# The router's products inside a recurrence's loop: weights stationary, tokens moving, four chunks on four column tiles

## The chip, the cores and the metric

One core of a Trainium2 chip runs the whole program. The time is device microseconds from start to end of an execution; the median of three is compared. All data is fp32 in HBM.

## The reference

One step of a one-layer streaming encoder for 512 new frames and 64 frames of a running stream (576 tokens, 5 tiles of at most 128). Cut to its course:

```python
h = rmsnorm(x, norm1_g)
proj = h @ w_in
att, k_new, v_new = swa_sink_attention(qa, ka, va, k_hist, v_hist, pos0, attn_sink)
rec, s_new = hgrn2(qb, fb, ib, gb, lb, hgrn_norm_g, s0)   # chunkwise recurrence, 4 heads of 128
x = x + jnp.concatenate([att, rec], axis=-1) @ w_o
h2 = rmsnorm(x, norm2_g)
g_logits = h2 @ w_rg + b_rg            # 4 groups
e_all    = h2 @ w_re + b_re            # 4 experts in each group: 20 columns in all
# top-1 group, top-2 experts in it, softmax weights
x = x + hier_moe(h2)                   # 16 experts, each 1024 -> 256 -> 1024
y = rmsnorm(x, final_norm_g)
```

What matters here is `h2 @ [w_rg | w_re]`: for each tile of 128 tokens a product over 1024 features, in 8 chunks of 128, with 20 result columns.

## The kernel before

The program is written by hand, engine by engine: every engine has its own list of instructions, in the order in which the code issues them, and semaphores join the lists. Each engine works its list strictly from front to back.

First come the input projections, then attention by chunks of 64 frames. Then a loop over token tiles, `t = 1` to `4`, joins three things: the recurrence of tile `t`, the product with `w_o` of tile `t - 1` (`out_part`, 16 units of three matmuls each, split in pieces to fill PE's time), and the second norm and the router of tile `t - 2`. Behind the loop the last two tiles are routed, tokens are gathered by expert, and the experts run.

On PE, a pass of the loop is: `turn_rec(t - 1)` (transposes the recurrence's result, L1898), `decays(t)`, `out_part` units 0 to 6, `inner(t)` (L1861, L1866), `turn_h2(t - 2)` (L1957), units 6 to 10, `sums(t)` (L1880, L1889), `route(t - 2)` (L1971), units 10 to 16. `out_part(t - 1)` begins only when DVE's `mix_low(t - 1)` is done (`rec_taken`).

On ACT, behind `sums(t)`: `rec_squares(t)` (L956), then in the next pass `mix_high` (L1000, L1002), `second_norm` (L988), `cum_exps` (L944 to L947), and `h2T_half` (L993), which copies half of the transposed h2 out of PSUM.

On POOL: the reciprocal roots (`rstd`, L663, L664), of the recurrence's rows (`ro`) and of the second norm.

On DVE, a pass ends and the next begins so:

```python
inner_and_states(t)      # L1283, L1302
h2T_half(t - 2)          # L1348, the other half of h2T
add_out(t - 1, 0)        # L1272
logf_low(t + 1)
take_logits(t - 2)       # L1359, waits for the router's products
normed(t)                # L1315, waits for POOL's ro
gain(t + 1)              # L1244, not in the last pass
pick(t - 2)              # L1378 to L1395: ranks the 20 logits
# next pass
add_out(t - 1, 1)        # L1272; t here is the new one less one
mix_low(t)               # L1453, L1456, waits for ACT's mix_high
```

Behind the loop PE issues five small products that rank the picked tokens (L1992, L1996), and then `out_part` of the last tile (its first matmul is L1942).

PSUM bank 7 holds both the router's logits (20 columns) and, in `inner`, the state update of a tile's first chunk, which DVE reads in `inner_and_states`; `route` therefore waits for `state_ready`. fp32 products are two records each on PE in the trace.

Of the kernel before, what the change touches and what calls it, by code (L numbers as in the profile page):

```python
# [24 lines left out]
ALU = mybir.AluOpType  # L25
ACT = mybir.ActivationFunctionType
# [5 lines left out]
P = 128  # L32
D = 1024
KC = D // P
SEQ, DEC = 512, 64
TOK = SEQ + DEC
NT = (TOK + P - 1) // P
PROMPT_TILES = SEQ // P
CHUNK = 64
NCHUNK = TOK // CHUNK  # L40
# [5 lines left out]
BW = BH * BK  # L46
EPS = 1e-6
NG, EPG = 4, 4
NE = NG * EPG
# [25 lines left out]
def rows_of(t):  # L75
    return min(P, TOK - t * P)
# [44 lines left out]
def program(nc, io):  # L121
    ctx = ExitStack()
    with ctx:
        def sem(name):
            return ctx.enter_context(nc.semaphore(name))
# [7 lines left out]
        def place(name, shape, dt=F32):  # L133
            n = int(np.prod(shape[1:])) * 4
            t = nc.alloc_sbuf_tensor_at(name, shape, dt, offset=cursor[0])
            cursor[0] += (n + 31) // 32 * 32
            return t
# [3 lines left out]
        ident = place("ident", [P, P])  # L141
# [13 lines left out]
        g2_bc = place("g2_bc", [P, D])  # L155
        ng_at = cursor[0]
        ng_bc = place("ng_bc", [P, BW])
        w_route = place("w_route", [P, KC, NG + NE])
        b_route = place("b_route", [P, NG + NE])
        sink_bc = place("sink_bc", [P, GROUP])  # L160
        stats = place("stats", [P, 6, 8])
# [105 lines left out]
        def hgrn_buffers(t):  # L267
# [8 lines left out]

        St = [hT_flat[:, 6 * BW:7 * BW], kT[:, 0:BW], V[:, 0:BW // KVW, :].rearrange("p t k -> p (t k)")]
        logf_parts = at("logf_parts", [P, 2, BW], F32R, hT_at + 7 * BW * 4)
        s_sample = bias[:, :, :].rearrange("p m k -> p (m k)")[:, 0:BW]

# [83 lines left out]
        h2_stored = sems("h2_stored", NT)  # L366
        h2_turned, h2T_act, h2T_dve, logits_ready, logits_taken = (
            sem(n) for n in ("h2_turned", "h2T_act", "h2T_dve", "logits_ready", "logits_taken"))
        route_diff, route_exp, picks_ready, rank_ready, hot_ready, slots_ready = (
            sem(n) for n in ("route_diff", "route_exp", "picks_ready", "rank_ready", "hot_ready", "slots_ready"))  # L370
        over_hot_ready, over_slots_ready, over_ready = (
# [268 lines left out]
        def _(pool):  # L640
# [86 lines left out]
            for c in range(NCHUNK):  # L727
                if c >= 2:
                    pool.wait_ge(scores_ready, c - 1)
                for b in range(KV):  # L730
# [3 lines left out]

                    pool.wait_ge(qbd_ready, KV * c + b + 1)

            for t in range(NT):
                rstd(0, t, BH, 1.0 / BK, osq_ready, ro_ready, osq[:, :], ro[:, :], rows_of(t))
                if t:
                    rstd(1, t - 1, 1, 1.0 / D, ssq2_ready, rstd2_ready)  # L740
# [83 lines left out]
        def _(act):  # L824
# [125 lines left out]
            def rec_squares(t):  # L950
                r = rows_of(t)
                act.wait_ge(rec_sum, t + 1)
                for h in range(BH):
                    cols = slice(h * BK, (h + 1) * BK)

                    last = act.activation(logf[0:r, t, cols], ps[0:r, 5, cols], ACT.Square,  # L956
                                          accum_out=osq[0:r, h:h + 1])
                last.then_inc(osq_ready, 1)
# [32 lines left out]
            def h2T_half(t):  # L991
                act.wait_ge(h2_turned, t + 1)
                act.activation(h2T[:, 0:512], bank(turned_bank(t)), ACT.Copy).then_inc(h2T_act, 1)  # L993
                if t >= NT - 2:
                    act.activation(h2T[:, 512:1024], bank(turned_bank(t) + 1), ACT.Copy).then_inc(h2T_act, 1)

            def mix_high(t):
                r = rows_of(t)
                act.wait_ge(rec_turned, t + 1)
                act.activation(mix_hi[:, BH:KC, 0:r], bank(6).rearrange("p (h t) -> p h t", h=BH)[:, :, 0:r],  # L1000
                               ACT.Copy).then_inc(mix_hi_done, 1)
                act.activation(mix_hi[:, 0:BH, 0:r], mixT[:, 0:BH, tok(t)], ACT.Copy).then_inc(mix_hi_done, 1)  # L1002
# [7 lines left out]
            for t in range(1, NT):  # L1010
                mix_high(t - 1)
                if t == 1:
                    high(len(W_GROUPS), 6, KC)
                else:
                    second_norm(t - 2)
                cum_exps(t)
                if t < NT - 1:
                    logf_high(t + 1)
                if t == 1:
                    high(len(W_GROUPS) + 1, 0, KC)  # L1020
                else:
                    h2T_half(t - 2)
                rec_squares(t)
            mix_high(NT - 1)
            second_norm(NT - 2)
# [42 lines left out]
            for t in range(NT):  # L1068
                r = rows_of(t)
# [615 lines left out]
        def _(pe):  # L1685
# [184 lines left out]
            def sums(t):  # L1870
                r = rows_of(t)
                _, _, qex, aT, _, _ = hgrn_buffers(t)
                pe.wait_ge(at_ready, t + 1)
                if t == NT - 1:
                    pe.wait_ge(s_in, 16)
                elif r > CHUNK:
                    pe.wait_ge(state_ready, 2 * t + 1)
                for h in range(BH):
                    cols = slice(h * BK, (h + 1) * BK)
                    pe.matmul(ps[0:r, 5, cols], aT[0:r, h, 0:r], vf[0:r, t, cols], start=h == 0, stop=True,  # L1880
                              skip_group_check=h > 0)

                for h in range(BH):
                    cols = slice(h * BK, (h + 1) * BK)
                    for c in range(r // CHUNK):
                        before = s_sample if t == NT - 1 else St[(2 * t + c) % 3]
                        rows = slice(c * CHUNK, (c + 1) * CHUNK)
                        if 2 * t + c:
                            last = pe.matmul(ps[rows, 5, cols], qex[:, h, rows], before[:, cols], start=False,  # L1889
                                             stop=True, skip_group_check=True)  # L1890
                last.then_inc(rec_sum, 1)
# [31 lines left out]
            def out_part(t, first, last_n):  # L1923

                r = rows_of(t)
                for n in range(first, last_n):
                    half, c = n // KC, n % KC
                    k = len(W_GROUPS) + half
                    if t == 0:
                        pe.wait_ge(w_lo_done, KC * k + c + 1)  # L1930
                    if c == 0:
                        if t == 0:
                            wait_emptied(pe, "g")
                            wait_emptied(pe, "b")
                        else:
                            pe.wait_ge(x2_ready, 2 * (t - 1) + half + 1)
                        pe.wait_ge(rec_taken, t + 1)
                    out, w_h, w_l = ps[0:r, half, :], w_high(k, c), w_lo[k % RING][:, c, :]
                    if t == NT - 1:
                        if c:  # L1940
                            pe.matmul(out, mix_hi[:, c, 0:r], w_l, start=False, stop=False)
                        last = pe.matmul(ps[:, half, :], mix_hi[:, c, :], w_h, start=c == 0, stop=c == KC - 1)  # L1942
                        if c == 0:
                            pe.matmul(out, mix_hi[:, c, 0:r], w_l, start=False, stop=False)
                    else:
                        pe.matmul(out, mix_hi[:, c, 0:r], w_h, start=c == 0, stop=False)  # L1946
                        pe.matmul(out, mix_hi[:, c, 0:r], w_l, start=False, stop=False)  # L1947
                        last = pe.matmul(out, mix_lo[:, c, 0:r], w_h, start=False, stop=c == KC - 1)  # L1948
                    if c == KC - 1:
                        last.then_inc(out_ready, 1)  # L1950
# [9 lines left out]

            def route(t):
                r = rows_of(t)
                pe.wait_ge(h2T_act, t + 1 + max(t - NT + 3, 0))
                if t < NT - 2:
                    pe.wait_ge(h2T_dve, t + 1)
                if t:
                    pe.wait_ge(logits_taken, t)

                pe.wait_ge(state_ready, min(2 * t + 5, 2 * PROMPT_TILES + 1))
                for c in range(KC):  # L1970
                    last = pe.matmul(ps[0:r, 7, 0:NG + NE], h2T[:, c * P:c * P + r], w_route[:, c, :],  # L1971
                                     start=c == 0, stop=c == KC - 1)
                last.then_inc(logits_ready, 1)

            for t in range(1, NT):
                early, late = (6, 12) if t == 1 else (6, 10)
                turn_rec(t - 1)
                decays(t)  # L1980
                out_part(t - 1, 0, early)
                inner(t)
                if t >= 2:
                    turn_h2(t - 2)
                out_part(t - 1, early, late)
                sums(t)
                if t >= 2:
                    route(t - 2)
                out_part(t - 1, late, 2 * KC)

            def rank_before(t):
# [22 lines left out]
                rank_own(t)  # L2014
            out_part(NT - 1, 0, 2 * KC)
            turn_h2(NT - 2)
            route(NT - 2)
            turn_h2(NT - 1)
            route(NT - 1)
            for t in range(NT - 3):  # L2020
                slots_of(t)
            pe.wait_ge(picks_ready, NT - 1)
# [122 lines left out]
```

## Time and profile before

| | |
|---|---|
| median of 3 runs | 491.68 us (491.62 to 493.36) |
| the profiled execution's own time | 491.68 us |
| its span, first to last instruction | 489.9 us |
| PE busy | 440.4 us, 90% |
| DVE busy | 250.1 us, 51% |
| ACT busy | 156.5 us, 32% |
| POOL busy | 91.9 us, 19% |
| PE, 40 products L1971 (five routings) | 9.3 us |
| granted clock of PE, 218 to 281 us | 1.00 |

Times are microseconds from the span's start. PE is matmul, PEld its weight loads, which run beside it. A matmul's end is modelled, and neighbouring matmuls overlap in the records; in the chain each is given the time until the next. "[idle before <-releaser]" is how long the engine stood idle ahead of the instruction, and who ended it. The passes of the loop that route a tile (t = 2, 3, 4) lie between 218 and 281 us.

### The profile page before, as it was taken

What the parts mean: (1) busy time and instruction counts of PE and PEld (TensorE: products, weight loads), DVE (VectorE), ACT (ScalarE), POOL (GpSimd) and SP (SyncE); (2) the same over time, 40 slices, a digit from 0 to 9 for tenths busy, and PEclk for the clock granted to TensorE, in tenths of its full rate; (3) what the DMA queues carried; (4) which work ended last, traced back from release to release, by engine and by line L of the source; (5) the groups of instructions that cost most, each with busy time, mean ns of one, the idle gap of its engine ahead of it and who ended that gap; (6) DMA issues with size and microseconds to landing.
All of it is one profiled execution on the core that took longest, in us unless ns stands there. A gap on an engine that the chain in (4) does not pass through costs nothing.

```text
span 489.9 us, 7956 instructions
## 1 busy us (share of the span) xinstructions
PE 440.4 (90%) x3093; PEld 304.1 (62%) x3093; DVE 250.1 (51%) x597; ACT 156.5 (32%) x355; POOL 91.9 (19%) x156
## 2 busy tenths in 40 slices
PE   6999899999999999999999989799999999998200
PEld 5879799887999678778888868333333433433000
DVE  4877715378568436776756468333312112111086
ACT  6664540375244653832413230111011111111021
POOL 4239100201000001010100023201211122122044
PEclk9999999999999999999999995999999999999755
DMA  8905401303000940051011099999999999950394
GB/s 299 224 16 174 172 9 26 146 1 137 36 2 9 255 153 1 22 173 44 0 44 66 1 349 418 343 415 343 397 372 399 424 413 417 416 212 34 122 343 180
DMA packets 31823, 93.18 MB, mean 190 GB/s; under 512 B 8969, under 2 KB 12177, under 8 KB 25649
## 3 DMA queue, kind: packets, MB, share of 16 engines
q1 hardware_dynamic: 27728, 82.81, 46.4%
q0 software_dynamic: 4064, 9.97, 5.3%
q8 instruction: 19, 0.31, 0.3%
q14 instruction: 12, 0.09, 0.1%
HBM read 85.75 MB, written 11.80 MB: 199 GB/s over the span
## 4 chain that ended last, share of the span: by engine, by line
PE 78%; DVE 10%; DMA 6%; ACT 3%; issue 1%; POOL 1%; SPq 0%; POOLq 0%; DVEq 0%; ACTq 0%
PE ps L2085 17%; PE ps L2064 8%; PE ps L1733 8%; PE ps L1735 7%; PE ps L1734 7%; PE ps L1946 3%; PE ps L2039 3%; PE ps L1948 3%; PE ps L1947 3%; DMA pair<-y_pairs 2%; DVE x L1664 2%; PE ps L1971 2%; DMA h_rows<-s_buf 1%; PE ps L1779 1%; ACT s_buf L927 1%
## 5 line engine op out<-in xcount | busy, mean ns | idle before, releaser
L2085 PE MATMUL ps<-we_gu,xT 128*32 128x512 f32 x768 | 84.9, 594 | 0.7 <-ACT xT L1038 0.6
L2085 PEld LDWEIGHTS ps<-we_gu,xT 128*32 128x32 f32 x768 | 24.5, 110 | 52.3 <-issue 50.2
L1733 PE MATMUL ps<-hT_hi,w_hi 128*128 128x288 f32 x160 | 48.5, 303 | 1.6 <-DVE w_lo_q L1108 0.8
L2064 PE MATMUL ps<-we_d,hhT 128*32 128x512 f32 x384 | 43.5, 592 | 1.3 <-DVE hhT L1649 1.3
L1640 DVE TENSOR_TENSOR hh<-sg,ps 128x256 f32<-128x256 f32 x12 | 5.1, 421 | 70.3 <-ACT sg L1054 70.3
L1733 PE MATMUL ps<-w_hi,hT_hi 128*128 128x512 f32 x96 | 38.8, 405 | 0.1
L1734 PE MATMUL ps<-w_lo,hT_hi 128*128 128x512 f32 x96 | 37.5, 390 | 0.0
L1733 PEld LDWEIGHTS ps<-hT_hi,w_hi 128*128 128x128 f32 x160 | 30.1, 188 | 5.0 <-issue 2.5
L1054 ACT ACTIVATE sg<-ps 128x256 f32<-128x256 f32 x12 | 4.6, 384 | 86.6 <-PE ps L2085 86.6
L2064 PEld LDWEIGHTS ps<-we_d,hhT 128*32 128x32 f32 x384 | 13.0, 110 | 29.0 <-issue 29.0
L854 ACT ACTIVATE w_hi<-ring,g_col 128x512 fp32r<-128x512 f32 (+1 forms) x48 | 28.7, 678 | 0.1
L1735 PE MATMUL ps<-hT_hi,w_lo 128*128 128x288 f32 x96 | 28.3, 295 | 0.0
L1111 DVE SCALAR_TENSOR_TENSOR w_lo<-ring,g_col,w_hi 128x512 fp32r<-128x512 f32 (+1 forms) x40 | 25.4, 701 | 0.0
L1625 DVE COPY y<-ps 128x512 f32<-128x512 f32 x12 | 8.3, 692 | 33.4 <-PE ps L2064 33.4
L1947 PE MATMUL ps<-w_lo,mix_hi 128*128 128x512 f32 x64 | 25.0, 390 | 0.0
L1734 PE MATMUL ps<-hT_lo_a,w_hi 128*128 128x288 f32 x80 | 23.6, 295 | 0.0
L1734 PE MATMUL ps<-hT_lo_b,w_hi 128*128 128x288 f32 x80 | 23.6, 295 | 0.0
L732 POOL COPY qbd<-qa 64x256 f32<-64x256 f32 x18 | 8.0, 444 | 80.6 <-PE ps L1779 44.7
L663 POOL TENSOR_SCALAR ms<-osq 128x4 f32<-128x4 f32 (+1 forms) x5 | 1.0, 193 | 110.6 <-ACT logf L956 110.6
L1733 PEld LDWEIGHTS ps<-w_hi,hT_hi 128*128 128x128 f32 x96 | 18.0, 188 | 5.7 <-issue 1.2
L2039 PEld LDWEIGHTS ps<-ident,xg 128*128 128x128 f32 x104 | 12.6, 194 | 13.1 <-issue 10.1
L1734 PEld LDWEIGHTS ps<-w_lo,hT_hi 128*128 128x128 f32 x96 | 18.1, 188 | 3.2
(389 smaller groups left out, 957.7 us busy)
## 6 DMA issues: line engine op xcount, KB each, us to landing
we_gu<-in_w_gate SPq DMA_DIRECT2D x16, 1024.0 KB, 9.2
we_gu<-in_w_up SPq DMA_DIRECT2D x16, 1024.0 KB, 11.0
we_d<-in_w_down SPq DMA_DIRECT2D x16, 1024.0 KB, 10.5
ring<-in_w_in SPq DMA_DIRECT2D x4, 2048.0 KB, 7.9
pair<-y_pairs SPq DMA_DIRECT2D x8, 512.0 KB, 7.6
ring<-in_w_in SPq DMA_DIRECT2D x3, 1024.0 KB, 8.2
x_first<-in_x_p SPq DMA_DIRECT2D x4, 512.0 KB, 9.8
x<-in_x_p SPq DMA_DIRECT2D x4, 512.0 KB, 3.7
```

Source lines behind the costliest of these rows:

```text
L854: act.activation(w_split(k, w_high(k, c)), w_raw(k, c), ACT.Copy, scale=gain).then_inc(w_hi_done, 1)
L1111: ins = dve.scalar_tensor_tensor(out, w_raw(k, c), g1_col[:, c:c + 1], hi, ALU.mult, ALU.subtract)
L1664: dve.scalar_tensor_tensor(x[0:r, t, :], pair[0:r, t, i * D:(i + 1) * D], gates[0:r, i, t:t + 1], x[0:r, t, :], ALU.mult, ALU.add).then_in ...
L1733: pe.matmul(out, stationary[0], moving[0], start=c == 0, stop=False)
L1734: pe.matmul(out, stationary[0], moving[1], start=False, stop=False)
L1735: last = pe.matmul(out, stationary[1], moving[0], start=False, stop=c == KC - 1)
L1946: pe.matmul(out, mix_hi[:, c, 0:r], w_h, start=c == 0, stop=False)
L1947: pe.matmul(out, mix_hi[:, c, 0:r], w_l, start=False, stop=False)
L1948: last = pe.matmul(out, mix_lo[:, c, 0:r], w_h, start=False, stop=c == KC - 1)
L2039: last = pe.transpose(ps[:, 1 + half, (c % 4) * P:(c % 4 + 1) * P], xg[:, b, c:D:KC], ident[:, :])
L2064: last = pe.matmul(ps[cols, 4 + 2 * (b % 2) + half, :], hhT[:, f, cols], we_d[u][:, f, 512 * half:512 * half + 512], start=f == 0, stop=f ...
L2085: last = pe.matmul(ps[cols, 0, :], xT[:, c, cols], we_gu[u][:, :, c, :], start=c == 0, stop=c == KC - 1)
```

## The change

In the three passes of the loop with a router, `route` no longer holds h2T (128 features x 128 tokens) as the stationary operand with the 20 weight columns moving. A chunk's weights are stationary, 32 columns read from a flat buffer (20 of the chunk, 12 of what follows), and the 128 tokens move. Chunks 0 to 3, then 4 to 7, go to four column tiles, so that four partial sums stand on partitions 0 to 31, 32 to 63 and so on of bank 7. ACT copies these out of PSUM (`take_parts`), and one more product (`route_sum`) with `pick_row`, a 128x20 matrix of ones and zeros, adds the four and gives the logits with tokens on partitions, as before. `route` moves ahead of `sums(t)`; `route_sum` stands behind it. The two routings behind the loop (`route_last`) stay as they were. POOL builds `pick_row` and clears the 12 added columns.

```diff
-        w_route = place("w_route", [P, KC, NG + NE])
+        w_route_flat = place("w_route_flat", [P, KC * (NG + NE) + 12])
...
+        bias_flat = bias[:, :, :].rearrange("p m k -> p (m k)")
+        s_sample = bias_flat[:, 0:BW]
+        parts, pick_row = bias_flat[:, BW:BW + P], bias_flat[:, BW + P:BW + P + NG + NE]
+        w_route = w_route_flat[:, 0:KC * (NG + NE)].rearrange("p (c n) -> p c n", c=KC)
...
+            pool.memset(w_route_flat[:, KC * (NG + NE):], 0.0)
+            pool.wait_ge(scores_taken, NCHUNK)
+            chain(pool.tensor_tensor(pick_row, ident[:, 0:20], ident[:, 32:52], ALU.add))
+            chain(pool.tensor_tensor(pick_row, pick_row, ident[:, 64:84], ALU.add))
+            chain(pool.tensor_tensor(pick_row, pick_row, ident[:, 96:116], ALU.add))
+            pool.sem_inc(consts, 1)
...
+            def take_parts(t):
+
+                r = rows_of(t)
+                act.wait_ge(parts_ready, t + 1)
+                if t:
+                    act.wait_ge(logits_ready, t)
+                act.activation(parts[:, 0:r], ps[:, 7, P:P + r], ACT.Copy).then_inc(parts_taken, 1)
...
                     h2T_half(t - 2)
+                    take_parts(t - 2)
                 rec_squares(t)
...
             def route(t):
                 r = rows_of(t)
-                pe.wait_ge(h2T_act, t + 1 + max(t - NT + 3, 0))
-                if t < NT - 2:
-                    pe.wait_ge(h2T_dve, t + 1)
+                pe.wait_ge(h2T_act, t + 1)
+                pe.wait_ge(h2T_dve, t + 1)
                 if t:
                     pe.wait_ge(logits_taken, t)
 
-                pe.wait_ge(state_ready, min(2 * t + 5, 2 * PROMPT_TILES + 1))
+                pe.wait_ge(state_ready, 2 * t + 5)
+                if t == 0:
+                    pe.wait_ge(consts, 3)
+                for k in range(2):
+                    for j in range(4):
+                        c = 4 * k + j
+                        last = pe.matmul(ps[32 * j:32 * j + 32, 7, P:P + r], w_route_flat[:, 20 * c:20 * c + 32], h2T[:, c * P:c * P + r],
+                                         start=k == 0, stop=k == 1)
+                last.then_inc(parts_ready, 1)
...
+            def route_sum(t):
+
+                r = rows_of(t)
+                pe.wait_ge(parts_taken, t + 1)
+                pe.matmul(ps[0:r, 7, 0:NG + NE], parts[:, 0:r], pick_row,
+                          start=True, stop=True).then_inc(logits_ready, 1)
...
                 out_part(t - 1, early, late)
+                if t >= 2:
+                    route(t - 2)
                 sums(t)
                 if t >= 2:
-                    route(t - 2)
+                    route_sum(t - 2)
                 out_part(t - 1, late, 2 * KC)
```

On PE, in the pass t = 3 of the loop, this is the end of `out_part`'s units 6 to 10, `sums(3)` and `route(1)` before.

```order
L1946 MATMUL ps<-wo_hi_h,mix_hi 128x512
L1947 MATMUL ps<-w_lo_106,mix_hi 128x512
L1948 MATMUL ps<-wo_hi_h,mix_lo 128x512
L1880 MATMUL ps<-vf,hT_f 128x128 [waits state_ready,at_ready]
L1880 MATMUL ps<-vf,hT_f 128x128 x3
L1889 MATMUL ps<-hT_f 64x128
L1889 MATMUL ps<-kT,hT_f 64x128
...
L1971 MATMUL ps<-w_route,pt 128x20 [waits logits_taken,state_ready,h2T_dve,h2T_act]
L1971 MATMUL ps<-w_route,pt 128x20 x7
L1946 MATMUL ps<-wo_hi_w,mix_hi 128x512
```

The same place in the changed program, whose lines are numbered further on (`pt` holds h2T, `bias` holds `parts` and `pick_row`).

```order
L1965 MATMUL ps<-wo_hi_h,mix_hi 128x512
L1966 MATMUL ps<-w_lo_106,mix_hi 128x512
L1967 MATMUL ps<-wo_hi_h,mix_lo 128x512
L1993 MATMUL ps<-pt,w_route_flat 32x128 [waits logits_taken,state_ready,h2T_dve,h2T_act]
L1993 MATMUL ps<-pt,w_route_flat 32x128 x7
L1899 MATMUL ps<-vf,hT_f 128x128 [waits state_ready,at_ready]
L1899 MATMUL ps<-vf,hT_f 128x128 x3
L1908 MATMUL ps<-hT_f 64x128
L1908 MATMUL ps<-kT,hT_f 64x128
...
L2011 MATMUL ps<-bias 128x20 [waits parts_taken]
L1965 MATMUL ps<-wo_hi_w,mix_hi 128x512
```

The eight products and their waits for h2T have moved from behind `sums` to ahead of it, and one product that waits for ACT stands in their old place.

On ACT, in the same pass of the changed program, the new copy (L1013) stands between the copy of h2T and the squares of the recurrence.

```order
L1003 ACTIVATE pt<-ps 128x512 [waits h2_turned]
L1013 ACTIVATE bias<-ps 128x128 [waits parts_ready]
L966 ACTIVATE logf,osq<-ps 128x128 [waits rec_sum]
L966 ACTIVATE logf,osq<-ps 128x128 x3
L1018 ACTIVATE mix_hi<-ps 128x512 [waits rec_turned]
```

Before, the rows of h2T's copy and of the squares were neighbours; the rest of ACT's row is in the same order. DVE's order is unchanged.

## Rows read from the trace of the kernel before

**Rows 1.** The page's head.
```profile
span 489.9 us, 7956 instructions
```
**Rows 2.** The chain that ended last, pass t = 2: start, us, what.
```profile
232.21 1.89 PE ps L1971 x16
...
238.29 0.45 PE ps L1898 x4
...
238.77 0.61 ACT mix_hi L1000
...
239.40 0.55 DVE mix_lo L1453
...
240.01 0.69 DVE mix_lo L1456
...
240.83 0.47 PE ps L1946
```
**Rows 3.** The same chain in the passes t = 3 and 4.
```profile
252.90 1.89 PE ps L1971 x16
...
261.51 0.48 PE ps L1946
...
273.36 1.89 PE ps L1971 x16
...
281.21 0.47 PE ps L1942
```
**Rows 4.** DVE in order of time: start, us, instruction, idle before and its releaser.
```profile
234.82 1.12 DVE L1315 SCALAR_TENSOR_TENSOR hT_f<-ps,ro,gg 128x128 f32<-128x128 f32 x4 [0.37 <-POOL ro L664]
...
238.29 0.17 DVE L1393 COPY before<-both 128x16 f32<-128x16 f32 x1
238.37 0.68 DVE L1272 TENSOR_TENSOR x<-x,ps 128x512 f32<-128x512 f32 x1
239.40 0.69 DVE L1453 TENSOR_TENSOR mix_lo<-ps,mix_hi 128x512 fp32r<-128x512 f32 x1 [0.34 <-ACT mix_hi L1000]
...
259.06 0.68 DVE L1272 TENSOR_TENSOR x<-x,ps 128x512 f32<-128x512 f32 x1
...
278.78 0.17 DVE L1395 TENSOR_TENSOR before<-before,both 128x16 f32<-128x16 f32 x1
...
280.31 0.42 DVE L1453 TENSOR_TENSOR mix_hi<-ps,mix_hi 128x256 fp32r<-128x256 f32 x1
```
**Rows 5.** Prices: PE's records, chain pieces, expert products and weight loads.
```profile
251.96 0.27 PE L1889 MATMUL ps<-hT_f 128*64 128x128 f32 x1
...
252.07 0.27 PE L1889 MATMUL ps<-hT_f 128*64 128x128 f32 x1
...
251.87 1.02 PE ps L1889 x16
...
245.21 0.89 PE ps L1861 x8
...
331.90 7.07 PE L2085 MATMUL ps<-we_gu,xT 128*32 128x512 f32 x64
...
331.90 0.16 PEld L2085 LDWEIGHTS ps<-we_gu,xT 128*32 128x32 f32 x8 [0.20 <-ACT xT L1038]
...
L2085 PEld LDWEIGHTS ps<-we_gu,xT 128*32 128x32 f32 x768 | 24.5, 110 | 52.3 <-issue 50.2
```
**Rows 6.** DVE's copy of h2T and the start of `sums` on PE, t = 2.
```profile
229.38 0.68 DVE L1348 COPY pt<-ps 128x512 f32<-128x512 f32 x1
...
230.14 1.05 PE L1880 MATMUL ps<-vf,hT_f 128*128 128x128 f32 x8
```
**Rows 7.** The first and last of the five rank products on PE.
```profile
279.78 0.40 PE L1996 MATMUL ps<-both,earlier 128*128 128x16 f32 x2
...
280.70 0.37 PE L1996 MATMUL ps<-both,earlier 128*128 128x16 f32 x2
```
**Rows 8.** POOL's first work after the score blocks.
```profile
193.51 0.20 POOL L663 TENSOR_SCALAR ms<-osq 128x4 f32<-128x4 f32 x1 [54.07 <-ACT logf L956]
```

More of the change, by code:

```diff
@@ L278, in program @@
         logf_parts = at("logf_parts", [P, 2, BW], F32R, hT_at + 7 * BW * 4)
-        s_sample = bias[:, :, :].rearrange("p m k -> p (m k)")[:, 0:BW]
+        bias_flat = bias[:, :, :].rearrange("p m k -> p (m k)")
+        s_sample = bias_flat[:, 0:BW]
+        parts, pick_row = bias_flat[:, BW:BW + P], bias_flat[:, BW + P:BW + P + NG + NE]
+        w_route = w_route_flat[:, 0:KC * (NG + NE)].rearrange("p (c n) -> p c n", c=KC)
         cursor[0] = after_small
@@ L368, in program @@
             sem(n) for n in ("h2_turned", "h2T_act", "h2T_dve", "logits_ready", "logits_taken"))
+        parts_ready, parts_taken = sem("parts_ready"), sem("parts_taken")
         route_diff, route_exp, picks_ready, rank_ready, hot_ready, slots_ready = (
@@ L1962, in route, with route_last @@
                 r = rows_of(t)
-                pe.wait_ge(h2T_act, t + 1 + max(t - NT + 3, 0))
-                if t < NT - 2:
-                    pe.wait_ge(h2T_dve, t + 1)
+                pe.wait_ge(h2T_act, t + 1)
+                pe.wait_ge(h2T_dve, t + 1)
                 if t:
                     pe.wait_ge(logits_taken, t)
-                pe.wait_ge(state_ready, min(2 * t + 5, 2 * PROMPT_TILES + 1))
+                pe.wait_ge(state_ready, 2 * t + 5)
[7 more added lines that the diff above has]
+                last.then_inc(parts_ready, 1)
+            def route_last(t):
+                r = rows_of(t)
+                pe.wait_ge(h2T_act, t + 1 + max(t - NT + 3, 0))
+                pe.wait_ge(logits_taken, t)
+                pe.wait_ge(state_ready, 2 * PROMPT_TILES + 1)
                 for c in range(KC):
@@ L1973, in route @@
                 last.then_inc(logits_ready, 1)
+            def route_sum(t):
+                r = rows_of(t)
+                pe.wait_ge(parts_taken, t + 1)
+                pe.matmul(ps[0:r, 7, 0:NG + NE], parts[:, 0:r], pick_row,
+                          start=True, stop=True).then_inc(logits_ready, 1)
             for t in range(1, NT):
@@ L2016, in _ @@
             turn_h2(NT - 2)
-            route(NT - 2)
+            route_last(NT - 2)
             turn_h2(NT - 1)
-            route(NT - 1)
+            route_last(NT - 1)
             for t in range(NT - 3):
```

## The prediction

> **What bounds the kernel now.** The page comes first: the span is 489.9 us [rows 1], and the profiled execution's own time is 491.68, so 1.78 lies around the span. That time is also the median of the three runs, so the sum below is made against 491.68.
>
> Next the chain that ended last, in the stretch that the edit touches. A pass of the loop over token tiles runs here from one product with `w_o` to the next. In the pass t = 2 the chain is PE without a break from the router's eight products (L1971, 1.89 us from 232.21) through the rest of `out_part` to the transposes of L1898 at 238.29, then ACT (L1000), DVE (L1453, L1456), and PE again at 240.83 [rows 2]. The passes t = 3 and t = 4 look the same: 252.90 to 261.51, and 273.36 to 281.21 [rows 3]. Let S be the end of `sums(t)`, where the router's products begin; the next `out_part` then begins 8.62, 8.61 and 7.85 us after S. A reader of the chain alone would take the router's 1.89 us three times, 5.67 us, as time on the path.
>
> The third view says what is late next: DVE's instructions in order of time. After S, ACT squares the sums, POOL makes the four scales, and DVE starts `normed` at 234.82, having waited 0.37 for POOL. From there it never stops: `normed`, `gain`, `pick`, then `add_out` at 238.37, and only then comes the wait before L1453, 0.34 us, for ACT [rows 4]. `mix_low` is behind all that on DVE's queue, and PE's next `out_part` waits for `mix_low`. So the chain by way of PE and ACT is ahead of a second one by a third of a microsecond only, and this second chain begins at S, not at the router.
>
> **The change, part by part.**
>
> *Ahead of S, PE gains work.* The new `route` (eight products of a 128x32 weight with 128 token columns) stands ahead of `sums(t)`, so it delays S. Each is two records on PE, as those of L1889 are; on four column tiles each tile has 2 products, 4 records. The nearest row is L1889, the same 128 columns in f32 on two column tiles: on one tile the records follow each other 0.11 us apart (251.96, 252.07), the two tiles side by side, and its 16 records take 1.02 us on the chain, of which 8 x 0.11 = 0.88 are records and 0.14 goes at the two ends [rows 5]. Four tiles side by side are seen in the experts' products: 64 records of 512 columns in 7.07 us, 0.11 each, while an unsplit 128-column record alone takes 0.89 / 8 = 0.111 [rows 5]; a quarter of the time per column. And eight weight loads of 32 columns are issued within 0.16 us there [rows 5]. So I take 4 x 0.11 + 0.14 = 0.58 us for a `route`. From below it is 0.44 (nothing at the ends), from above 1.02 (16 records at L1889's whole pace). Three passes: 1.74, between 1.32 and 3.06.
>
> `route` now also waits ahead of `sums` for DVE's copy of h2T. In the pass t = 2 that copy starts at 229.38 and takes 0.68, ending at 230.06; `sums` started on PE at 230.14 [rows 6]. The copy follows PE's `inner` by DVE's own work, so both ends move together: 0.08 us are left, and I price the wait at nothing. If the signal comes later than that, `sums` and all behind it wait by the excess, perhaps 0.1 a pass; this lies inside the bound of 1.02.
>
> *After S, PE loses work.* The old `route`, 1.89, goes; `route_sum` comes, one product with 20 columns, two records like those of L1971: 2 x 1.89 / 16 = 0.24. So PE reaches its transposes 1.65 us sooner after S. `route_sum` waits for ACT's copy of 128x128 from PSUM; a copy of four times the columns takes 0.61 [rows 2], and `sums` covers it from `route`'s end until S, 232.21 - 230.14 = 2.07 us. ACT has nothing else to do then: `rec_squares`, queued behind the copy, waits for S.
>
> *What DVE makes of it.* `logits` now come 0.24 after S and not 1.89, but DVE takes them ahead of `normed`, which waits for POOL until 2.61 after S, as before. So DVE's row keeps its place relative to S: `add_out` starts 238.37 - 232.21 = 6.16 after S (259.06 - 252.90 = 6.16 in t = 3), and `mix_low` can follow 0.61 later, as L1456 follows L1453 (239.40 to 240.01, [rows 2]), at 6.77. From there to PE's `out_part` it was 240.83 - 239.40 = 1.43. So the next `out_part` begins 8.20 after S where it began 8.62 and 8.61: 0.42 and 0.41 are saved, not 1.65. PE will have turned and run its decays by then and waits about a microsecond, where it waited hardly at all.
>
> In t = 4 there is no `gain`, and DVE was waiting for PE before `add_out`. The last operation of `pick` starts at 278.78 [rows 4]; the next can start 0.08 later (238.29 to 238.37), 5.50 after S, `mix_low` at 6.11, and PE's `out_part` 281.21 - 280.31 = 0.90 later, 7.01 after S against 7.85: 0.84 saved. The five small rank products ahead of it on PE wait for `pick` too; they take 280.70 + 0.37 - 279.78 = 1.29 [rows 7], from 278.95 - 273.36 = 5.59 to 6.88, just in time.
>
> *On POOL* four small operations come after the score blocks, where it sat idle for 54.07 us [rows 8]; without that cover they would cost well under 2 us once. The 12 added columns move buffers by 64 bytes: nothing.
>
> **The sum.** +1.74 - 0.42 - 0.41 - 0.84 = +0.07: 491.75, given as 491.8. With the two bounds of `route`: 491.68 + 1.32 - 1.67 = 491.3, and 491.68 + 3.06 - 1.67 = 493.1. Behind the loop everything starts from the last `out_part` (its products, the last two routings, the gather and the weight loads that wait for `mix_low`), so the shift is carried to the end unchanged.
>
> **Rivals.**
> *The PE chain's gain arrives in full.* Each pass would lose 1.89 - 0.24 - 0.58 = 1.07, in all 3.2: 488.5. For it: the chain names PE and nothing of DVE's `pick`. Against it: only 0.34 of idle stands before L1453. It would need `mix_low` to come ahead of `pick`.
>
> *Weight loads aren't hidden.* Each record would wait for its own load, 0.110 us [rows 5]: 4 x (0.110 + 0.11) + 0.14 = 1.02 a pass, +1.39, 493.1. Against it: L1889's records on one tile are 0.11 apart although each has a load of its own. The Trainium skill ("TensorE: Matmul & The Clock Gate", section "Part 3: Packing small matmuls — row/col tiling", "The mechanism") says that a weight load overlaps running products only where the row group differs, and the four tiles here share all rows; it would give this rival's time. The spacing of L1889 speaks against that rule on two tiles; no run here shows it on four with so few columns.
>
> *The tiles run one after another* (the other side). 16 x 0.111 + 0.14 = 1.92 a pass ahead of S, 5.76 - 1.67 = +4.1: 495.8. It ends slower by over 0.5% as soon as `route` takes over (2.46 + 1.67) / 3 = 1.38. Against it are the experts' rows, for it only that these have 512 columns.
>
> **How the numbers follow.** About 0.5% (2.5 us) is what a measurement of this kernel can tell from no change. The forecast gets 0.72, the full gain 0.10 (faster), loads not hidden 0.08 (within 0.5%), tiles in turn 0.07 (slower); the last 0.03, a late h2T copy or a rank product that pushes further, I count as slower. So faster 0.10, same 0.80, slower 0.10. The range goes from 490.5 (the sum's lower bound, less 0.3 a pass should DVE's stretch shrink by its 0.37 wait for POOL) to 493.4 (the upper bound, and the highest of the runs of before).
>
> **What would show it.** `route` at about 0.6 us of PE ahead of the products of `sums`; DVE with no idle before L1453's instruction in t = 2 and 3; the first product of `out_part` waiting some 1.2 us for DVE's `mix_low`; passes about as long as before (20.7 us, as from 240.83 to 261.51). It is wrong if DVE still waits for ACT there, or if `route` takes over a microsecond.

## The result and the profile after

The changed kernel takes 495.24 us, median of 20 runs; the kernel before, in 20 runs with it, 493.46. The ratio is 1.0036, 95% interval 1.0020 to 1.0052: slower by about 1.8 us (1.0 to 2.6). The three runs of before from which the forecast started lay low, with a median of 491.68; the forecast was a change of +0.1 us, and the measured one is +1.8. The profiled execution of the changed kernel took 493.59 us, with a span of 491.8.

The chain that ended last, in the pass t = 2 of the changed kernel (its line numbers; start, us, what):

```profile
229.99 0.57 PE ps L1993 x16
230.56 1.09 PE ps L1899 x8
231.65 1.05 PE ps L1908 x16
...
232.72 1.15 ACT logf L966 x8
...
234.23 1.03 POOL ro L668
...
235.29 1.13 DVE hT_f L1334 x4
...
238.38 0.27 DVE picks L1407 x2
...
239.44 0.68 DVE mix_lo L1472
240.13 0.61 DVE mix_lo L1475
...
240.87 0.47 PE ps L1965
```

The chain no longer runs through PE behind `sums`, as in [rows 2]. It leaves PE at S = 232.70 and comes back only at 240.87, having gone through ACT's squares, POOL's scales and DVE's `normed`, `gain`, `pick`, `add_out` and `mix_low`. The new `route` (L1993) is cheap, 0.57 us for 16 records.

DVE in order of time, at the place of [rows 4]:

```profile
238.85 0.68 DVE L1291 TENSOR_TENSOR x<-x,ps 128x512 f32<-128x512 f32 x1
239.44 0.68 DVE L1472 TENSOR_TENSOR mix_lo<-ps,mix_hi 128x512 fp32r<-128x512 f32 x1
```

No idle stands before L1472 now. The wait has gone to PE, as its waits from 218 to 283 us show (who waited for whom: us in total, times, longest):

```profile
PE ps L1965 <- DVE mix_lo L1475: 2.7, 3, 1.3
PE ps L2037 <- DVE before L1414: 0.8, 1, 0.8
```

The kernel before, in the same stretch:

```profile
PE ps L1946 <- DVE mix_lo L1456: 0.5, 2, 0.2
```

In these rows the loop has hardly changed. Its ends and the pieces of `sums`, in the chain of before:

```profile
220.20 0.47 PE ps L1946
...
230.30 0.89 PE ps L1880 x8
231.19 1.02 PE ps L1889 x16
...
271.32 1.01 PE ps L1880 x8
```

and in the chain of the changed kernel:

```profile
219.88 0.48 PE ps L1965
...
252.63 1.05 PE ps L1908 x16
...
261.83 0.47 PE ps L1965
...
272.22 1.01 PE ps L1899 x8
273.23 1.03 PE ps L1908 x8
...
281.26 0.47 PE ps L1961
```

From the first `out_part` product of the pass t = 2 to that of the last tile it took 281.21 - 220.20 = 61.01 us, now 281.26 - 219.88 = 61.38. That is +0.37 and not +1.8; the rest needs another explanation, and the experiments were made to find it.

Between these two profiles the rest of the difference lies behind the loop, which took 210.5 us to the end and 208.7 before. The copy of h2 to memory took 8.34 us against 7.32, and the experts began at a granted clock of 0.50 (311.3 to 314.6 us), where before's profile has 1.00. Before, and then the changed kernel (in its stretch the granted clock stands third from the end):

```profile
296.77 7.32 DMA h_rows<-s_buf
```

```profile
296.85 8.34 DMA h_rows<-s_buf
...
311.30:314.60 3.30, 3.30 (x19) 1.50 (x21) 1.86 (x5) 1.88 (x2) 0.99 (x1) 0.50 0.85 294
```

But two profiles of the next section, of the kernel before with moved buffers and with `pick` later, have the same two things: 8.01 and 8.23 us, and a granted clock of 0.50 from 312.8 to 316.0 and from 309.7 to 316.4. So this pair of profiles alone doesn't say what the change costs.

### The profile page after: what moved, and what is told of

Read it like the earlier page. It is cut to its first block, busy times and chain, and to the rows that moved or that the text cites. A ratio compares the mean times of both kernels' runs of the same rounds, so it can differ in the third digit from the quotient of the medians.

```text
span 491.8 us, 7978 instructions
## 1 busy us (share of the span) xinstructions
PE 440.6 (90%) x3099; PEld 301.8 (61%) x3099; DVE 249.6 (51%) x597; ACT 157.6 (32%) x358; POOL 93.1 (19%) x160
## 4 chain that ended last, share of the span: by engine, by line
PE 73%; DVE 13%; DMA 6%; ACT 4%; issue 2%; POOL 1%; SPq 0%; POOLq 0%; DVEq 0%; ACTq 0%
PE ps L2126 17%; PE ps L2105 8%; PE ps L1752 8%; PE ps L1754 7%; PE ps L1753 7%; PE ps L2080 3%; PE ps L1965 2%; PE ps L1967 2%; PE ps L1966 2%; DMA h_rows<-s_buf 2%; DMA pair<-y_pairs 2%; DVE x L1683 2%; PE ps L1798 1%; ACT s_buf L937 1%; DVE w_lo_q L1127 1%
## 5 line engine op out<-in xcount | busy, mean ns | idle before, releaser
L2126 PE MATMUL ps<-we_gu,xT 128*32 128x512 f32 x768 | 85.9, 600 | 0.4 <-ACT xT L1057 0.4
L1063 ACT ACTIVATE y<-ps 128x512 f32<-128x512 f32 x12 | 7.2, 598 | 39.1 <-PE ps L2105 39.1
```

What stands on the lines that cost most here:

```text
L2126: last = pe.matmul(ps[cols, 0, :], xT[:, c, cols], we_gu[u][:, :, c, :], start=c == 0, stop=c == KC - 1)
```

## The experiments

**Moved buffers alone.** The kernel before, with what stands behind the router's weights 64 bytes further on.

```diff
         w_route = place("w_route", [P, KC, NG + NE])
+        cursor[0] += 64
```

> The kernel before with all buffers behind the router's weights moved by 64 bytes, as the change moves them; nothing else. Inside the loop the changed kernel lost about 0.4 us, but its median lies 1.8 us above. Theory 1 (the remaining 1.4 us come with the time at which the expert stage starts, its clock and its transfers): the moved addresses alone cost nothing, ratio 1.000 within 0.001, and the passes of the loop are as before. Rival (the moved addresses make the transfers slower, as the copy of h2 to memory, 8.3 us after and 7.3 before, might say): ratio about 1.003, the transfers from and to SBUF about a tenth longer.

Ratio 0.9994 (0.9978 to 1.0011); loop 61.02 us. The addresses cost nothing that shows.

**The change without moved buffers.**

```diff
-        w_route_flat = place("w_route_flat", [P, KC * (NG + NE) + 12])
-        b_route = place("b_route", [P, NG + NE])
+        w_route_flat = place("w_route_flat", [P, (KC + 1) * (NG + NE)])
+        b_route = w_route_flat[:, KC * (NG + NE):]
...
-            pool.memset(w_route_flat[:, KC * (NG + NE):], 0.0)
```

> The change without moved buffers and without clearing 12 columns: the last chunk's 12 extra columns are the router's bias, which stands behind the weights anyway and meets zeros in the summing product. Theory 1: as the change, ratio 1.002 to 1.005. Rival (moved addresses): most of the loss is gone, ratio 1.000 to 1.001.

Ratio 1.0042 (1.0024 to 1.0059): as slow as the change. The two together rule moved addresses out.

**The new products behind the sums.**

```diff
-                if t >= 2:
-                    route(t - 2)
                 sums(t)
                 if t >= 2:
+                    route(t - 2)
+                    out_part(t - 1, late, late + 2)
                     route_sum(t - 2)
+                    late += 2
                 out_part(t - 1, late, 2 * KC)
...
-                    take_parts(t - 2)
                 rec_squares(t)
+                if t > 1:
+                    take_parts(t - 2)
```

> The changed form of the router's products, but behind the recurrence's sums where they stood before: sums, the eight products, two units of out_part, the summing product, the rest of out_part; on ACT the partial sums are copied behind the squares. So S, the end of sums, is not delayed. Theory 1 (S is delayed by about 0.8 us a pass, and what PE saves behind S is capped at 0.42 in t = 2 and 3 and 0.88 in t = 4 by DVE's row from normed to mix_low): the delay goes, the capped gain stays, the loop from the first out_part to the last one is 1.7 us shorter than before and 2 us shorter than the changed kernel, ratio about 0.997. Rival (the four-tile form itself is what costs, by its changes of tiling on PE, wherever it stands): no better than the change, ratio 1.002 to 1.004.

Ratio 0.9976 (0.9959 to 0.9994); loop 59.28 us, 1.73 below before and 2.10 below the change. The form on four tiles pays where it doesn't delay S.

**`pick` later.** In the changed kernel, DVE's `pick` of the tiles 0 and 1 stands behind `make_h2` of the next pass.

```diff
                     make_h2(t - 2)
+                    if t >= 3:
+                        pick(t - 3)
                 inner_and_states(t)
...
-                if t >= 2:
+                if t == NT - 1:
                     pick(t - 2)
```

> The change, with DVE's pick of the tiles 0 and 1 moved behind make_h2 of the next pass, where DVE stands idle for some 2 us; pick of the tile 2 stays. Theory 1 (pick, 1.9 us ahead of mix_low on DVE's queue, holds PE's saved time back): mix_low waits for PE and ACT again, PE's next out_part begins about 7.1 us after S and not 8.15, so about 1 us less in each of two passes, 2 us less than the changed kernel, ratio about 0.999 to 1.000. Rival (PE waits for POOL's scales and the turned rows, whatever DVE does in between): 8.15 stays, ratio as of the change, 1.003.

Ratio 0.9978 (0.9960 to 0.9995), better than expected; loop 59.24 us. The chain behind S, t = 2, in this kernel:

```profile
233.03 0.33 PE ps L2013 x2
...
237.59 0.45 PE ps L1919 x4
...
238.07 0.61 ACT mix_hi L1018
...
238.70 0.55 DVE mix_lo L1472
...
240.13 0.47 PE ps L1967
```

S is 233.03, and `out_part` follows 7.10 us later, by way of PE and ACT, where it was 8.17 in the change: `pick` on DVE's queue was what held PE back.

**The same move in the kernel before.**

> The kernel before with the same move of DVE's pick, router's products as they were. Theory 1 (before the change PE's chain through the router's products ended last, and DVE's row was 0.34 us ahead of it): nothing to gain, the next out_part still 8.6 us after S, ratio 0.999 to 1.000. Rival (moving pick pays by itself, whatever the router's form): the passes become about 1 us shorter as in the changed kernel, ratio 0.996.

Ratio 1.0001 (0.9980 to 1.0022), loop 60.98 us: nothing, as expected. Before the change PE's own chain ended last.

**Both moves.** Products behind the sums and `pick` later.

> Both of the two moves: the new products behind the sums, and pick of the tiles 0 and 1 behind make_h2 of the next pass. Theory 1: S isn't delayed, and mix_low waits for PE's and ACT's chain, not for pick: the next out_part about 7.6 us after S in t = 2 and 3 against 8.62 before and 8.2 with the products behind the sums alone; the loop 1.1 us shorter than with that alone, ratio about 0.995 to 0.996. Rival (what DVE has to do behind make_h2 then holds inner_and_states and the copy of h2T back): no better than either move, 0.997 to 0.998.

Ratio 0.9929 (0.9908 to 0.9951), loop 58.25 us, in six runs: a version faster than both kernels, by 3.5 us than before, where a ratio of 0.995 to 0.996 was expected. From S at 232.37 to `out_part` at 240.04 it takes 7.67 us.

**The old form in the new place.** The eight products as before, h2T stationary, ahead of `sums`.

```diff
+                if t >= 2:
+                    route(t - 2)
                 sums(t)
-                if t >= 2:
-                    route(t - 2)
```

> The kernel before with its eight products as they were, h2T stationary, moved ahead of the recurrence's sums. Theory 1 (where the router's products stand decides, since DVE's row from S to mix_low has a fixed length): S is 1.9 us later in each pass, the next out_part still 8.15 us after S, the loop 61.01 + 3 x 1.89 - 1.83 = 64.9 us, ratio 1.008, and up to 1.011 if the clock falls in PE's waits. Rival (the place is neutral, and the form of the products is what costs): ratio 1.000 to 1.002.

Ratio 1.0110 (1.0086 to 1.0135) in six runs, loop 64.77 us against 64.9 expected. The place is dear, and the new form pays for most of it.

**More products ahead of the experts**, on the kernel before and on the change.

```diff
-            for _ in range(30):
+            for _ in range(46):
```

> The kernel before with 46 instead of 30 products that keep PE going while the gathered rows are awaited ahead of the experts. Theory 1 (part of the changed kernel's loss comes from PE's clock falling to half in that wait, in more executions than before): the wait is short enough that the clock stays at full; 1 us or less gained on the kernel before, ratio 0.998 to 1.000, and less spread. Rival (the loss has nothing to do with the clock): ratio 1.000.

> The changed kernel with the same 46 products. Theory 1: the loss that isn't in the loop, about 1.4 us, is gone: this kernel is 0.3 to 0.5 us slower than the kernel before with 46 products, ratio to it 1.001. Rival (something else behind the loop is slower in the changed kernel, its transfers or its instructions): 1.8 us slower still, ratio to the kernel before with 46 products 1.0035.

Before: 0.9976 (0.9958 to 0.9995). The change: 1.0019 (1.0000 to 1.0037). Their medians lie 2.1 us apart (492.51 and 494.61), no less than without: theory 1's second half, that the loss sits at the experts' start, does not hold. In both profiles the experts begin at full clock (granted clock 1.00 from 311 to 317 us in the one, 312.5 to 319 in the other), and what follows the loop takes as long in the one as in the other (209.3 and 209.1 us). The second is longer in the loop, 62.84 us against 61.00: its pass t = 4 takes 13.85 us from the first `out_part` to S, and 12.43 in the changed kernel's own profile. PE there, in order of time (idle before and its releaser in brackets):

```profile
262.07 0.76 PE L1965 MATMUL ps<-wo_hi_top,mix_hi 128*128 128x512 f32 x1 [1.19 <-DVE mix_lo L1475]
262.63 0.63 PE L1966 MATMUL ps<-w_lo,mix_hi 128*128 128x512 f32 x1
263.06 0.63 PE L1967 MATMUL ps<-wo_hi_top,mix_lo 128*128 128x512 f32 x1
...
265.16 0.39 PE L1966 MATMUL ps<-w_lo,mix_hi 128*128 128x512 f32 x1
```

The same products take 0.63 us and then 0.39. The stretches of that profile (start and end, length, busy us and instructions of PE, PEld, DVE, ACT and POOL, granted clock, DMA share, GB/s):

```profile
258.00:262.00 4.00, 2.88 (x20) 2.09 (x19) 3.72 (x14) 2.36 (x5) 0.01 (x1) 0.96 0.00 0
262.00:265.00 3.00, 2.93 (x7) 2.38 (x8) 2.75 (x6) 1.19 (x4) 1.00 (x2) 0.50 0.00 0
265.00:268.00 3.00, 3.00 (x16) 2.22 (x16) 0.29 (x1) 0.00 (x0) 0.00 (x0) 0.98 0.62 220
```

```profile
279.95 0.40 PE L2036 MATMUL ps<-both,earlier 128*128 128x16 f32 x2 [0.76 <-DVE before L1413]
...
280.00:281.30 1.30, 1.24 (x10) 1.16 (x11) 1.30 (x5) 0.78 (x1) 0.00 (x0) 0.95 0.00 0
281.30:283.00 1.70, 1.70 (x4) 1.14 (x5) 1.19 (x6) 0.37 (x2) 0.90 (x2) 0.50 0.33 39
283.00:285.00 2.00, 2.00 (x7) 1.31 (x6) 1.06 (x1) 0.00 (x0) 0.00 (x0) 0.60 0.97 410
```

There the last tile's `out_part` takes 290.44 - 281.30 = 9.14 us against 288.89 - 281.26 = 7.63 in the changed kernel's own profile. So one such fall costs 1.4 to 1.5 us. That made theory 2: the new waits of PE aren't free, since some executions lose their clock in them or just behind.

**The waits filled.** The changed kernel with idle products in PE's waits.

```diff
                 decays(t)
+                if t >= 3:
+                    pe.wait_ge(logits_taken, t - 2)
+                    stay_busy(5)
                 out_part(t - 1, 0, early)
...
             turn_rec(NT - 1)
+            pe.wait_ge(logits_taken, NT - 2)
+            stay_busy(3)
             pe.wait_ge(picks_ready, NT - 2)
```

> The changed kernel with five idle products (identity by identity, 128 columns, 1.1 us in all) behind decays in the passes t = 3 and 4, and three before the rank products, where PE now waits for DVE's mix_low or pick; nothing waits for them. Theory 2 (the 1.2 us of PE's new wait in a pass let its granted clock fall to half in some executions, as it stood at 0.61 from 262 to 266 us in the changed kernel with 46 products, and at 0.68 from 282 to 286 in the one without moved buffers; that is the loss that isn't in the row of instructions, about 1.4 us): the waits are as long for the program, but the clock stays at full; the loop takes 61.4 us and the median falls by 1 to 1.4 us to a ratio of 1.000 to 1.0015. Rival (the loss comes with the expert stage, whose clock and transfers vary anyway): as the change, 1.0035 to 1.004.

Ratio 0.9997 (0.9978 to 1.0015); loop 61.42 us. The path in the loop is as long as the change's, yet the loss is gone, and the interval lies below that of the change (1.0020 to 1.0052) and of the change without moved buffers (1.0024 to 1.0059). The granted clock says the same. Each execution lists its mean over the whole span; it is 0.9483 on average over the 20 of the change, 0.9542 over the 12 with the waits filled, and 0.9523 over the 81 of before that the experiments list. The stretches of the filled kernel's profile, same columns:

```profile
258.00:262.00 4.00, 4.00 (x30) 3.29 (x29) 3.79 (x14) 2.25 (x5) 0.00 (x0) 1.00 0.00 0
262.00:265.00 3.00, 3.00 (x16) 2.46 (x14) 2.68 (x7) 1.30 (x5) 1.01 (x2) 1.00 0.02 5
```

**Both moves and 46 products.**

> The new products behind the sums, pick of the tiles 0 and 1 behind make_h2 of the next pass, and 46 instead of 30 products ahead of the experts. Expected by both theories: the gain of the two moves, 0.7%, and that of the longer run of products, 0.24%, add up, ratio 0.990 to 0.992; if they share a cause, 0.993.

Ratio 0.9926 (0.9906 to 0.9946), loop 58.24 us: no more than the two moves alone, so the longer run of products adds nothing to them that can be measured.

The kernels side by side. The measured change is the ratio's distance from 1 times 493.5 us, each good to about 0.9 us (1.2 for the old form in the new place); for the change with 46 products it is against the kernel before with 46. "Loop" is the change of the 61.01 us in its profile (for the change with 46 products the change's own, since a fall of the clock lies in its profile). "Rest" is the measured change less the loop's. "Clock" is the granted clock, averaged over the kernel's executions, less the same of before's executions beside it (for the change the 81 just named, for the change with 46 products the kernel before with 46); each is good to about 0.002.

| kernel | measured | loop | rest | clock | PE's longest wait in the loop |
|---|---|---|---|---|---|
| old form, new place | +5.4 | +3.8 | +1.7 | -0.0041 | 1.6 |
| the change | +1.8 | +0.4 | +1.4 | -0.0040 | 1.3 |
| the change, no moved buffers | +2.1 | +0.3 | +1.7 | -0.0039 | 1.3 |
| the change, 46 products | +2.1 | +0.4 | +1.7 | -0.0032 | 1.3 |
| the change, `pick` later | -1.1 | -1.8 | +0.7 | -0.0029 | 0.8 |
| products behind the sums | -1.2 | -1.7 | +0.5 | -0.0023 | 0.7 |
| the change, waits filled | -0.1 | +0.4 | -0.6 | +0.0017 | 0.2 |
| before, buffers moved | -0.3 | 0.0 | -0.3 | -0.0005 | 0.2 |
| before, `pick` later | 0.0 | 0.0 | +0.1 | -0.0011 | 0.2 |
| both moves | -3.5 | -2.8 | -0.7 | +0.0016 | 0.2 |

What the rows of the loop don't explain goes with PE's longest wait in it, and with the granted clock of all executions, not of the profiled ones alone. Among the 20 executions of the change, too, time and clock go together: the two lowest clocks, 0.942 and 0.943, belong to the two longest times, 499.79 and 498.23 us, and the eight at 0.950 or above took 492.72 to 495.64. By estimate, 0.0040 of 492 us is 3.9 us at half clock, a little more than one of the falls above in each execution.

## Why the prediction was right and wrong

*The price of `route`* was right: 0.57 us against 0.58. The rival "weight loads aren't hidden" fell with it. 16 loads, each 0.106 to 0.110 us long, went by within 0.57 us of products. The rule that the prediction named for that rival, that a load overlaps running products only where the row group differs (the Trainium skill, "TensorE: Matmul & The Clock Gate", section "Part 3: Packing small matmuls — row/col tiling", "The mechanism") doesn't hold for these four column tiles, and the measurement decides. That the tiles run in turn fell as well.

*What comes ahead of S* was sized too small: 0.81 and 0.74 and not 0.58 in the passes t = 2 and 3, since `sums` itself got longer behind the narrow products. Its first eight records, whose start [rows 6] shows, took 0.89 us in the chain of before (230.30 to 231.19) and take 1.09 now. From `out_part` to S it was 232.21 - 220.20 = 12.01 us in t = 2 and is now 232.70 - 219.88 = 12.82. In t = 4, where these records take 1.01 us in both kernels, it cost 0.58. Three passes together cost 2.1 and not 1.74.

*What is saved behind S* was right: the next `out_part` begins 240.87 - 232.70 = 8.17 us after S (8.20 foreseen), in t = 3 at 261.83 - 253.68 = 8.15, and in t = 4 at 281.26 - 274.26 = 7.00 (7.01 foreseen). The move of `pick` shows the cause directly: worth 2.1 us in the changed kernel's loop, and nothing in the kernel before. The rival that the PE chain's gain arrives in full fell.

All the signs that the prediction named came: `route` at 0.6 us, no idle before DVE's `mix_low`, PE's waits of 1.3 and 1.2 us, passes of 21 us. The time was off all the same.

*The step that failed* is "PE will have turned and run its decays by then and waits about a microsecond, where it waited hardly at all". The wait came just so, 1.3 us. I priced it at nothing, as idle time of an engine that isn't awaited; the sum has no term for it. But what PE does behind that wait is on the path, and it ran at half clock where the clock had fallen. Two of the three profiles of the change with its waits as they are (its own, without moved buffers, with 46 products) show a fall in the loop, of 1.4 to 1.5 us each, one in the wait for `mix_low` and one behind the wait for `pick`; the changed kernel's own profile shows none and lies low among its runs (493.59 against a median of 495.24). None of the profiles with waits of 0.2 us shows one in the loop. Filling the waits raises the granted clock and takes the loss away without shortening the loop. So of the 1.8 us measured the rows of the loop explain 0.4, 0.3 more than the sum had, and the 1.4 that the sum lacked goes to the clock.

*The starting point* was luck of the wrong kind. The sum began at 491.68, the median of three runs; 20 runs of the same kernel gave 493.46, which is itself above the upper end of the stated range, 493.4. Of the 3.4 us between the forecast time and the measured one, 1.8 came from there. (The lower end of the range, by its own terms 491.3 less 0.9, is 490.4 and not 490.5; nothing hangs on that.)

What stays open: how many of the falls lie in the loop. An execution that only has a time lists its mean granted clock, but not where it fell, and in some profiles the clock also falls at the experts' start, in those of the kernel before with moved buffers and with `pick` later too. The profiles of the old form in the new place (waits up to 1.6 us), of the products behind the sums and of the change with `pick` later show no fall in the loop but one at the experts' start, so the rest of these three is not located. For the change itself, the loop as the place is inferred from the two profiles with a fall, the pair with 46 products and the filled waits; it is not counted.

## What to carry to other kernels

Before shortening the chain that ended last, find the one that ends next, and start both at the event that they share: here both begin at the end of `sums`, and a step put ahead of that event delays both, while one taken away behind it shortens one. Faster work that only lets PE arrive early at a wait can cost time, if the clock falls in it or behind it; either shorten what is waited for, or keep PE busy. And when a result is off by more than the rows of the stage show, take a few more profiles of kernels with the same feature before blaming a stage that varies anyway, and compare the granted clocks of all executions, not only their times.

## What the runs showed of the hardware

A wait of PE of 1.19 us in the loop, where the granted clock stood at 1.00 before, ended in one profile at a granted clock of 0.50, which lasted about 3 us; in another profile the same came 1.2 us behind a wait of 0.76 us, with five products of 16 columns in between; other waits of 0.7 to 1.6 us in the loop were followed by no fall. Such a fall cost 1.4 to 1.5 us. Products of 128 columns on four column tiles, each with its own 32-column weights, went at 0.036 us a record, 16 in 0.57, three times as fast as the 0.111 of a record that fills the array; the first full-array products behind them took 1.09 us in place of 0.89 (t = 2 and 3), while the first products of `sums` in t = 4, on 64 rows and 64 columns, took 1.01 in both kernels.
